# A two-layer diffusion mixer: the next group's weights split ahead into places of their own, scale rows written after a transposition, and an earlier first scale

## The reference, cut to what matters

```python
for l in range(DEPTH):                       # DEPTH = 2
    sh1, sc1, ga1, sh2, sc2, ga2 = split(silu(c) @ w_mod[l] + b_mod[l], 6)   # c, and c_ctx for context
    u = rmsnorm(h, g_pre_mix) * (1 + sc1) + sh1
    y = mixers(u)        # 4 kinds of attention, gated, summed, then @ w_out
    h = h + ga1 * rmsnorm(y, g_post_mix)
    u = rmsnorm(h, g_pre_ffn) * (1 + sc2) + sh2
    h = h + ga2 * rmsnorm(swiglu(u), g_post_ffn)      # [1024 -> 2 x 2816 -> 1024]
```

## Time and profile before

| | |
|---|---|
| Time, median of 3 runs (lowest, highest) | 1852.48 us (1849.21, 1855.95) |
| The profiled execution: its time, its span | 1859.26 us, 1857.5 us |
| Granted TensorE clock, mean | 0.982 of full speed |
| PE busy, share of the span | 1762.4 us, 95% |
| DVE, ACT, POOL busy | 1154.3 us (62%), 873.7 us (47%), 585.8 us (32%) |
| DMA, mean over the span | 121 GB/s |

### The profile page before, as it was taken

How to read it: one execution, slowest core, us unless ns; L and a number is a source line. 1 busy time by engine, 2 the same in 40 slices (tenths; PEclk the granted TensorE clock), 3 DMA queues, 4 the chain that set the end, 5 groups by cost and what they waited for, 6 DMA issues and landing times. The chain is left out here.

```text
span 1857.5 us, 30572 instructions
## 1 busy us (share of the span) xinstructions
PE 1762.4 (95%) x10179; PEld 1496.8 (81%) x10179; DVE 1154.3 (62%) x2371; ACT 873.7 (47%) x1904; POOL 585.8 (32%) x555
## 2 busy tenths in 40 slices
PE   6999999999999999899999999888999999999998
PEld 3777788778788787788888887777898788979997
...
DMA packets 344453, 224.14 MB, mean 121 GB/s; under 512 B 57782, under 2 KB 322284, under 8 KB 344300
## 3 DMA queue, kind: packets, MB, share of 16 engines
...
## 5 line engine op out<-in xcount | busy, mean ns | idle before, releaser
L2035 PE MATMUL bank<-Uhi,w_ring 128*128 128x512 f32 (+1 forms) x1536 | 547.9, 357 | 18.6 <-ACT H L1700 7.4
L2036 PE MATMUL bank<-Ulo,w_ring 128*128 128x512 f32 (+1 forms) x1536 | 532.2, 347 | 0.0
L2037 PE MATMUL bank<-Uhi,w_ring 128*128 128x512 f32 (+1 forms) x1536 | 532.2, 346 | 0.0
L1561 ACT ACTIVATE w_ring<-load_ring 128x512 fp32r<-128x512 f32 (+3 forms) x632 | 369.9, 607 | 146.6 <-PE bank L2037 105.1
L1781 DVE TENSOR_TENSOR w_ring<-load_ring,w_ring 128x512 fp32r<-128x512 f32 (+1 forms) x424 | 317.9, 766 | 178.8 <-ACT w_ring L1561 153.1
L2035 PEld LDWEIGHTS bank<-Uhi,w_ring 128*128 128x128 f32 x1536 | 294.9, 192 | 60.1 <-ACT H L1700 10.5
L1516 POOL TENSOR_TENSOR w_ring<-load_ring,w_ring 128x512 fp32r<-128x512 f32 (+3 forms) x208 | 246.5, 1190 | 264.9 <-ACT w_ring L1561 148.9
L2037 PEld LDWEIGHTS bank<-Uhi,w_ring 128*128 128x128 f32 x1536 | 294.9, 192 | 36.3
L2036 PEld LDWEIGHTS bank<-Ulo,w_ring 128*128 128x128 f32 x1536 | 295.3, 192 | 30.0
L1504 POOL TENSOR_TENSOR Y<-Y,small 128x512 f32<-128x512 f32 x160 | 173.1, 1082 | 289.8 <-DVE small L1981 274.5
L1986 DVE TENSOR_TENSOR Z<-bank,Z 128x512 fp32r<-128x512 f32 x160 | 109.6, 685 | 98.2 <-ACT Z L1686 97.4
...
## 6 DMA issues: line engine op xcount, KB each, us to landing
load_ring<-in_w_in SPq DMA_DIRECT2D x192, 256.0 KB, 2.9
load_ring<-in_w_ffn_in SPq DMA_DIRECT2D x160, 256.0 KB, 3.2
mod_ring<-in_w_mod SPq DMA_DIRECT2D x96, 256.0 KB, 3.2
load_ring<-in_w_ffn_out SPq DMA_DIRECT2D x88, 256.0 KB, 3.3
mod_place<-in_w_mod SPq DMA_DIRECT2D x64, 256.0 KB, 2.8
load_ring<-in_w_branch SPq DMA_DIRECT2D x64, 256.0 KB, 2.9
...
load_ring<-in_w_in SPq DMA_DIRECT2D x64, 128.0 KB, 2.5
```

Of the source, the lines that this page charges most:

```text
L1561: act.activation(w_ring[:, plan.slot['w', key], 0, 0:sz], load_ring[:, plan.slot['load', key], 0:sz], ACT.Copy).then_inc(sem['w_hi'], 1)
L2035: pe.matmul(dst, lhs[0], rhs[0], start=start, stop=False)
L2036: pe.matmul(dst, lhs[0], rhs[1], start=False, stop=False)
L2037: return pe.matmul(dst, lhs[1], rhs[0], start=False, stop=stop)
```

## The change

Five things are changed.

1. **Splits ahead.** The eight pieces of the first product after a boundary (`('first', l, 'ffn')` and `('first', 1, 'mix')`) leave `w_ring` and get places in `Z`, at the start of the area of the attention outputs or of the FFN's hidden values, free when the last piece before the passes is used. Their splits are steps `early_split`: one behind each of the first four pieces of pass 0, two more after the new `h` of tile 0, and the last two later in the passes. In B1 and B2 the pieces that follow the group are no longer split four ahead during it, but only from right position 5 on.
2. **All left, then all right.** In `begin` with 4 token tiles, the left 256 tokens go through all eight `kt`, then the right 256. The hooks of tiles 2 and 3 are spread over positions 0 to 5 (before: 0 to 4), and one half of tile 2's `h` moves ahead of the loop. For the left side of `kt` 3 and 5 the scale runs on DVE (`apC`), and ACT only rounds. The transposition banks take turns in another order.
3. **Scale rows by transposition.** PE transposes each [128 x 8] tile into a bank, ACT copies [8 x 128] out of it and writes it to DRAM in 8 rows of 512 B. In layer 1 both rows share one bank, so PE's second transposition waits for ACT's first copy; in layer 0 a row takes a place in the ring `acc`.
4. **Small vectors sooner.** The 24 small DMAs move ahead of the last three `w_mod` pieces.
5. **First scale sooner.** Tiles 2 and 3 of x are turned before `par`, and tile 0 is scaled before tiles 4 to 7 are turned.

```diff
+SCALED_BY_DVE = ((0, 3), (0, 5))
@@ ModPlan.add_up
             p.step('coef', (0, 1 if ch < 24 else 2))
+            p.take('acc', ('row', (0, int(ch >= 24))), ('row_copied', (0, int(ch >= 24))))
             p.step('rowput', (0, int(ch >= 24)), sides=2)
@@ build_plan
-        ring = ('b3', 'pv', 'b4')[p.turns % 3]
-        p.turns += 1
+        ring = ('b3', 'b4', 'pv')[(side * KT + kt) % 3]
@@ begin
-        parts = [('gmm_a', 0, kt) for kt in range(W_RING)] + [('gmm_b', 1, kt) for kt in range(W_RING)] if both else \
-            [('gmm', 0, kt) for kt in range(W_RING)]
-        parts += [('gmm', 0, kt) for kt in range(W_RING, KT)]
+        parts = [('gmm_a' if both else 'gmm', 0, kt) for kt in range(KT)] + [('gmm_b', 1, kt) for kt in range(KT * both)]
...
+                kind = 'apC' if both and (side, kt) in SCALED_BY_DVE else 'apA'
...
     p.step('mod0row', 0)
+    turn_in(range(2, 4))
...
     first_columns(0)
-    turn_in(range(2, KT))
+    normed((nm, 0, 0), 0, 0, None, NTOK)
+    turn_in(range(4, KT))
@@ output
                 for g in range(2):
+                    p.take('modf', ('row', (l + 1, g)), ('row_copied', (l + 1, g)))
                     p.step('rowput', (l + 1, g), sides=1)
...
-            passes(0, 0, W_RING)
+            if nxt:
+                p.early[nxt] = ('piece_used', (key, early - 1))
+            for kt in range(W_RING):
+                passes(0, kt, kt + 1)
+                if nxt and kt < 4:
+                    early_split(nxt, kt + 1)
             y_sum(nmo, 1, 0)
             y_scale(nmo, 0)
             h_both(nmo, 0)
+            if nxt:
+                early_split(nxt, 6)
...
                 u_next(nmo, 0)
                 h_stat(nmo, 1)
+                early_split(nxt, KT)
                 passes(1, 2, W_RING)
                 p.step('warm', nmo, times=WARM)
                 u_next(nmo, 1)
...
             passes(3, 0, 2)
+            early_split(nxt, 7)
             y_sum(nmo, 1, 2)
             u_next(nmo, 1)
+            early_split(nxt, KT)
             y_scale(nmo, 2)
+            h_new(nmo, 2, 0)
             passes(3, 2, 3)
...
-                    0: [lambda: h_new(nmo, 2, 0), lambda: y_sum(nmo, 1, 3), lambda: h_new(nmo, 2, 1)],
-                    1: [lambda: y_scale(nmo, 3), lambda: h_sums(nmo, 2), lambda: h_stat(nmo, 2)],
-                    2: [lambda: h_both(nmo, 3), lambda: u_next(nmo, 2)],
-                    3: [lambda: h_sums(nmo, 3), lambda: h_stat(nmo, 3)],
-                    4: [lambda: u_next(nmo, 3)]}
+                    0: [lambda: h_new(nmo, 2, 1)],
+                    1: [lambda: y_sum(nmo, 1, 3), lambda: y_scale(nmo, 3)],
+                    2: [lambda: h_sums(nmo, 2), lambda: h_stat(nmo, 2), lambda: h_both(nmo, 3)],
+                    3: [lambda: u_next(nmo, 2)],
+                    4: [lambda: h_sums(nmo, 3), lambda: h_stat(nmo, 3)],
+                    5: [lambda: u_next(nmo, 3)]}
@@ the order of the splits
+        if st[0] == 'early':
+            while done < len(use) and (use[done][0] != st[1] or use[done][1] < st[2]['upto']) and (
+                    use[done][0] in p.early or ringed[place[use[done]] - W_RING] in used):
+                done = split()
+            continue
...
+            ahead = AHEAD if st[0] not in ('gmm_a', 'gmm_b') else 1 + max(0, st[1][1] - 4) if st[0] == 'gmm_b' else 1
@@ sync
-            first_mod(0)
+            first_mod(0, range(5))
...
                 sp.dma_start(sink[:, l, :], sink_b[l:l + 1, :].to_broadcast([P, 8])).then_inc(s_rows, 16)
+            first_mod(0, range(5, KT))
@@ scalar
-                    act.wait_ge(sem['coef_ready'], count['coef_ready', (l, 1 + g)])
-                    for side in range(f['sides']):
-                        act.dma_start(gain_kept[l, g, side].rearrange("(k p) -> p k", p=P),
-                                      coef[:, l, 1 + 2 * g, :, side],
-                                      allow_slow_non_contiguous=True).then_inc(s_put[l][g], 16)
+                    act.wait_ge(sem['row_turned'], count['row_turned', key])
...
+                    act.activation(gain_turned[:, at:at + ns, :], row_bank(key)[0:KT, 0:ns * P].rearrange("k (s p) -> k s p", s=ns),
+                                   ACT.Copy).then_inc(sem['row_copied'], 1)
+                    act.wait_ge(sem['row_copied'], count['row_copied', key])
+                    for side in range(ns):
+                        act.dma_start(gain_kept[l, g, side].rearrange("(k p) -> k p", p=P),
+                                      gain_turned[:, at + side, :]).then_inc(s_put[l][g], 16)
@@ vector
+                elif kind == 'apC':
...
+                    dve.tensor_scalar(fil[:, plan.slot['fil', ('ap', key)], 0:SEQ], ut_bank(f['bank'])[:, 0:SEQ],
+                                      is_ab(f['l'], 2 * f['which'])[:, kt, side:side + 1], shift(f['l'], f['which'], kt, side),
+                                      ALU.mult, ALU.add).then_inc(sem['ap_made'], 1)
@@ tensor
+                elif kind == 'rowput':
...
+                    pe.wait_ge(sem['coef_ready'], count['coef_ready', (l, 1 + g)])
+                    for side in range(f['sides']):
+                        ins = pe.transpose(row_bank(key)[0:KT, side * P:(side + 1) * P], coef[:, l, 1 + 2 * g, :, side], ident)
+                    ins.then_inc(sem['row_turned'], 1)
```

118 lines of the change are left out of this document (75 added, 43 removed).

## The result

| | before | after |
|---|---|---|
| Time, median of 6 runs each (lowest, highest) | 1852.74 us (1849.21, 1855.95) | 1860.49 us (1857.23, 1861.31) |
| Ratio after to before, 95% interval | | 1.0035 (1.0023 to 1.0047) |
| The profiled execution: its time, its span | 1859.26 us, 1857.5 us | 1861.31 us, 1859.5 us |
| PE busy | 1762.4 us | 1761.9 us |
| DVE, ACT, POOL busy | 1154.3, 873.7, 585.8 us | 1160.4, 874.4, 587.6 us |

The change makes the kernel 7.75 us slower by the medians and 6.5 us (1.0035) by the ratio; I had forecast 6.4 us faster. The two profiled spans differ by only 2.0 us, because the execution profiled before was 6.5 us above its median and the one after 0.8 us above its own.

What follows compares the result with a forecast made beforehand. PE, busy 95% of the span, was taken as the bound, leaving some 95 us of idle and half-clock time. B1 -2.9, B2 -1.2, B3 -0.9, layer 0 rows +1.0, start -2.4 sum to -6.4: 1846.1 us, range 1835 to 1858.

Steps and rivals of the forecast that it cites:

- the chain is counted from rows of this very stretch: B1: reason for taking the inner value, -2.9 us, between bounds of -7.2 and +0.6.
- rival (c): Boundaries: PE stops at `un` of tile 1, then runs products at half clock; +8.1 us, 1860.6; chance 0.15.
- the 2.2 us of wait that were to stay in the loop: B1 loop: normed tile 3 needs 10.5 us, PE has 8.3 us of work; wait mostly at position 3.
- the sum above takes the usual durations: B1, B2: POOL splits priced as not stretching DVE; four meetings at 0.8 us would leave only some 1 us together.
- The 1.6 us for `issue`: B2: PE's wait read as caused by crawling early loads, which writing 8 rows of 512 B ends.
- the split that held `un` stays in the same place, now for piece 6, ... `un` comes 1.0 us later: B3: the DVE split of 1.54 us before `un` of tile 1 stays; `un` 1.0 us later.
- rival (d): Passes' late splits: `w_ring` could hold them back, so fewer than eight are early; given no chance of its own.
- the squares of tile 0 wait for a load as at B1: B3: ACT's squares of tile 0 wait for an early piece's load; at B1 this made them 1.7 us late.
- PE waits elsewhere in attention, which can swallow it: Layer 0's scale rows: reason for taking +1.0 us between 2.1 us and nothing.
- where PE has had pieces 0 to 4 for a while: the last piece's products end 1.8 us later: Start: `w_mod` piece 5 lands near 20.0 us behind the small DMAs, ending the last products 1.8 us later.
- the first scale runs beside four transpositions: Start: this ordering removes PE's wait of 1.86 us for the first scaled tile.
- the clock's lower level grows from B1's 5 us: Sign that the forecast is wrong: the low-clock time grows from B1's 5 us to more, favouring rival (c).

Runs made afterwards that it cites:

- b_rows_layer1: The kernel before with only layer 1's two scale rows turned and written as 512-byte rows; B2 takes 95.9 us, no gain.
- a_rows_bytes: The changed kernel with the scale rows again written in 4-byte elements, without transposition on PE; ratio 1.0070 to the kernel before.
- a_dve: The changed kernel with the low parts of all early splits on VectorE; ratio 1.0024 to the kernel before.
- c_dve: The changed kernel, early loop stopped at piece eight, later early splits with low parts on VectorE, old start, layer 0's rows in 4-byte elements; ratio 0.9996 to before.

## Why the prediction was wrong

By the stretches the start is 3.5 us worse than forecast, B3 3.4, B1 1.9 and the scale rows of layer 0 0.9; B2 came out as forecast. The two largest are steps that had the wrong sign.

**B1, forecast -2.9, came out at -0.6 to -1.4 us.** The step "the chain is counted from rows of this very stretch" was right in kind: `un` of tile 1 late (1.7 us forecast, 2.4 measured), ACT waiting for the load of early piece 3 (it does, 1.8 us, until 764.32), and a single long stop. Three terms were mis-sized. The stop took 3.8 us instead of 2.4. The sum priced every product at 1.66 us, the upper clock, though rival (c) had the other: from 776.2 to 783.0 PE is at 1.2 GHz and loses 2.9 us. Before, it lost 2.4 us there, so the clock got only some 0.5 us worse; what failed is that the sum let it go to nothing. Against these two, the 2.2 us of wait that were to stay in the loop came out at 0.5. And "the sum above takes the usual durations" was the wrong choice between row and rule. Row 1655.37 showed a DVE split at twice its length, and B1 of the kernel before had a new `h` of tile 3 that took 2.43 us for two where 1.40 is usual, with a POOL split beside it:

```profile
776.31 2.43 DVE L1880 SCALAR_TENSOR_TENSOR H<-Y,row_stat,H 128x512 f32<-128x512 f32 x2
...
776.76 1.43 POOL L1516 TENSOR_TENSOR w_ring<-load_ring,w_ring 128x512 fp32r<-128x512 f32 x1
```

Four such meetings at 0.8 us were my own estimate of the rule's price, and here the split took 1.79 us for 0.69 and `un` 1.88 for 0.88. The Trainium skill, SBUF — State Buffer, section "SBUF: two separate sides", says of the pair of ports that GpSimd and VectorE share that it is an exclusive lock: whichever starts first has it for its whole instruction, and the other is fully blocked. The rows agree, to 0.2 us: POOL's split of 775.62 ends at 776.88, 1.20 us after `un` begins; with the usual 0.88 us behind it that makes 2.08 us, and 1.88 were measured. For the split of 768.40, beside POOL's of 768.25, it makes 1.93 us against 1.79. By the page this holds for an instruction with one SBUF input too, if VectorE runs it in a mode that takes both ports; `un` has one such input and was stretched; its mode stands in no trace.

**B2, forecast -1.2, came out at -1.2 us**, in part by luck. The crawl went, the stop at `un` took 3.5 us for the nearly 4 forecast, and `un` of tile 1 came 3.7 us later for 4.3. But the turned rows cost PE 0.6 us of waits where I had 1.3, and the clock, at nothing in the sum, was low for 6.8 us instead of 3.4, some 1.1 us more lost. The 1.6 us for `issue`, which I had read as the crawl's, were the stop itself (b_rows_layer1). Which of the parts wins it I had not told apart. a_rows_bytes and b_rows_layer1 show that neither part gains alone: early splits without the transposition lose 12 us, the transposition without early splits wins nothing. Behind B2 both profiles of after are 0.5 to 2.7 us shorter than before's; a_dve, with B2 the same to 0.2 us, is at 308.9. What decides it was not tested.

**B3, forecast -0.9, came out at +2.4 to +2.6 us.** The failed step is "the split that held `un` stays in the same place, now for piece 6, ... `un` comes 1.0 us later". The 2.0 us for the silu went, as forecast. But three splits stand in that place, one early (0.69) and two from the overrun (2.36). I had read the loop's condition for rival (d), whether *fewer* than eight are early, and not whether it stops. The step "the squares of tile 0 wait for a load as at B1" was mis-sized: 1.7 us there, 3.7 us here, and PE stops 2.3 us for `un` of tile 0. And to let an early split cost what the ring's split cost misses POOL: with the overrun cut out, B3 is the same 185.7, since 1.0 us goes to contention, 1.2 to the later silu product and 1.1 to the clock, and the stop for tile 0 stays. Late order and no POOL together bring it to 180.2, with the clock at its upper level throughout, and to 181.5 in c_dve, where it is low for 3.4 us: the gain that I had looked for, and twice to three times its size.

**Scale rows in layer 0, forecast +1.0 (0 to 2.1), measured +1.9**: waits of 0.56 and 1.10 us and two transpositions of about 0.13 each. The terms were right (1.1, 0.75 and 0.3 us in the forecast); the discount for "PE waits elsewhere in attention, which can swallow it" was not. At an equal time at the lower clock the kernels without them are 2.1 us faster in L0.

**Start, forecast -2.4 (0 to -3.5), came out at 0 in the first profile, about +1 over all.** The failed step is "where PE has had pieces 0 to 4 for a while: the last piece's products end 1.8 us later". Piece 5 is waited for until 21.38 and `coef` comes 3.1 us later (31.45 for 28.32). The step "the first scale runs beside four transpositions" forgot that ACT also copies tiles: behind its scaling they hold PE for 1.33 us. And the bound of 0 was no bound.

Rival (c) named the mechanism, its place and nearly the total (1860.6), but the total is luck: it had B1 at +0.6 and B2 at +3.5, where both got faster, and only B3 (+1.8) and the rows (+2.2) came near. Its sign, "the clock's lower level grows from B1's 5 us", did not come at B1, where it is 6.8 us in both kernels, but at B2. Its 0.15 was too little. A stop of PE in front of products, priced by my own count at 2.4 and 4 us, should have put the clock's price into the forecast itself.

What stays open: by the stretches the start, L0 and B3 cost +1.1, +1.9 and +2.5 us and B1 and B2 win 1.0 and 1.2, a sum of +3.3, where the runs say +5.7 to +7.8. So 2.4 to 4.5 us have no place in the profiles. These are two executions of each kernel, and not typical ones: the first of before was 6.5 us above its median, and the means of the two spans differ by only 1.8 us.
